# A hybrid decoder step on one core: the last down projection in two passes over token halves

## What is computed

```python
def conv_ffn(h, conv_hist, w_gate, w_up, conv_w, conv_b, w_down):
    gt = h @ w_gate
    ext = jnp.concatenate([conv_hist.astype(gt.dtype), gt], axis=1)
    c = conv_b
    for j in range(CONV_W):
        c = c + ext[:, j:j + L] * conv_w[j]
    f = jax.nn.gelu(c, approximate=True) * (h @ w_up)
    return f @ w_down, ext[:, L:]
...
    f, new_conv = conv_ffn(rmsnorm(x, lp['g_ffn_pre']), ...)
    x = x + rmsnorm(f, lp['g_ffn_post'])
```

## Time and profile before

| | us |
|---|---|
| runs: median of 3 (lowest to highest) | 2643.88 (2643.35 to 2646.94) |
| the profiled execution | 2648.2 |
| its span, first to last instruction | 2646.5 |
| last down projection on PE | 2557.3 to 2605.4 |
| last residual add of DVE ends | 2643.4 |

### The profile page before, as it was taken

How to read it: one execution, slowest core, us unless ns; L and a number is a source line. 1 busy time by engine, 2 the same in 40 slices (tenths; PEclk the granted TensorE clock), 3 DMA queues, 4 the chain that set the end, 5 groups by cost and what they waited for, 6 DMA issues and landing times.

```text
span 2646.5 us, 52869 instructions
## 1 busy us (share of the span) xinstructions
PE 2525.7 (95%) x20496; PEld 2398.3 (91%) x20496; DVE 1127.3 (43%) x1842; ACT 684.2 (26%) x1188; POOL 120.9 (5%) x265
## 2 busy tenths in 40 slices
PE   8999998789899987999999999999999999999994
PEld 8999997555579987999999999999999999999994
DVE  6532313512253339543444344434444444434357
ACT  5211112511022224322222222222222222222231
POOL 3000000000000005000000000000000000000002
PEclk9999998999999998999999999999999999999997
DMA  5478775088864322223323222232323232323231
GB/s 170 133 263 279 274 265 205 1 307 335 320 229 165 87 75 56 85 83 92 88 87 87 87 87 87 87 87 87 87 84 91 87 87 83 91 87 87 83 97 75
DMA packets 146625, 347.36 MB, mean 131 GB/s; under 512 B 16608, under 2 KB 16608, under 8 KB 146048
## 3 DMA queue, kind: packets, MB, share of 16 engines
q1 hardware_dynamic: 144480, 338.35, 39.4%
q0 software_dynamic: 2080, 8.14, 0.8%
HBM read 334.32 MB, written 12.10 MB: 131 GB/s over the span
## 4 chain that ended last, share of the span: by engine, by line
PE 85%; SPq 5%; DVE 4%; DMA 3%; issue 1%; ACT 1%; DVEq 1%; POOL 0%; ACTq 0%
PE ps_acc L719 30%; PE ps_acc L696 15%; PE ps_a L719 15%; PE ps_b L719 15%; PE ps_a L771 4%; SPq L341 3%; SPq L345 1%; DMA region<-vcache 1%; DMA w_raw<-units 1%; PE ps_a L696 1%; PE ps_b L696 1%; PE ps_acc L826 1%; DMA region<-kcache 1%; DVE act_lo L988 1%; PE ps_a L882 1%
## 5 line engine op out<-in xcount | busy, mean ns | idle before, releaser
L270 DVE TENSOR_TENSOR w_lo<-w_raw,w_hi 128x512 fp32r<-128x512 f32 x724 | 500.0, 702 | 1148.6 <-ACT w_hi L264 1144.9
L264 ACT ACTIVATE w_hi<-w_raw 128x512 fp32r<-128x512 f32 x724 | 445.5, 628 | 1432.3 <-PE ps_acc L719 474.6
L719 PE MATMUL ps_acc<-act_hi,w_hi 128*128 128x272 f32 x1472 | 308.9, 292 | 24.7 <-DVE act_lo L988 18.0
L719 PE MATMUL ps_acc<-act_lo,w_hi 128*128 128x272 f32 x1472 | 307.4, 290 | 0.0
L719 PE MATMUL ps_acc<-act_hi,w_lo 128*128 128x272 f32 x1472 | 305.5, 289 | 0.0
L696 PE MATMUL ps_acc<-act_hi,w_hi 128*128 128x272 f32 x1280 | 273.6, 295 | 0.5 <-ACT q_dec L532 0.5
L696 PE MATMUL ps_acc<-act_hi,w_lo 128*128 128x272 f32 x1280 | 264.5, 288 | 0.0
L696 PE MATMUL ps_acc<-act_lo,w_hi 128*128 128x272 f32 x1280 | 264.0, 288 | 0.0
L719 PEld LDWEIGHTS ps_acc<-act_hi,w_hi 128*128 128x128 f32 x1472 | 233.2, 190 | 27.3 <-issue 12.8
L719 PEld LDWEIGHTS ps_acc<-act_hi,w_lo 128*128 128x128 f32 x1472 | 234.1, 190 | 0.0
L719 PEld LDWEIGHTS ps_acc<-act_lo,w_hi 128*128 128x128 f32 x1472 | 233.8, 190 | 0.0
(11 more groups left out here) (217 smaller groups left out, 3725.0 us busy)
## 6 DMA issues: line engine op xcount, KB each, us to landing
w_raw<-units SPq DMA_DIRECT2D x724, 256.0 KB, 2.6
region<-kcache SPq DMA_DIRECT2D x128, 512.0 KB, 4.4
region<-vcache SPq DMA_DIRECT2D x128, 512.0 KB, 7.4
region<-xT SPq DMA_DIRECT2D x8, 544.0 KB, 6.9
region<-xT SPq DMA_DIRECT2D x4, 1088.0 KB, 8.4
yT<-region SPq DMA_DIRECT2D x8, 544.0 KB, 2.7
ext_out<-region POOLq DMA_DIRECT2D x8, 339.5 KB, 3.9
kT_out<-scratch POOLq DMA_DIRECT2D x8, 272.0 KB, 6.4
```

Source lines behind the costliest of these rows:

```text
L264: act.activation(w_hi[:, s], w_raw[:, s], ACT.Copy).then_inc(hi_ready, 1)
L270: dve.tensor_tensor(w_lo[:, s], w_raw[:, s], w_hi[:, s].bitcast(F32), ALU.subtract).then_inc(lo_ready, 1)
L719: mm = pe.matmul(banks(mt, odd)[:, n, 0:HN], w[:, s, i, cols], half(a[:, kt], n), start=kt == 0 and w is w_hi and a is hi, stop=kt == 2 * ...
```

## The change

The last chunk's down projection (16 units) is written out instead of looped, and runs twice, over tokens 0 to 271 and then 272 to 543. In the first pass each unit is split into a place of its own that is kept: the first four in the ring, the other twelve in the space of `act_hi` and `act_lo`, which nobody needs by then. The second pass reads them there. The first pass takes the quarters in pairs (`DOWN`): the four units of `f` tiles 0 and 1 first, then the four of `f` tiles 2 and 3; quarters with even `d` use the first bank of each pair, odd ones the second. The second pass takes them in their old order and uses only the second banks.

All that follows a tile goes by halves too: adds into `acc`, squares (now with four buffers, `sq4`), square sums, root, diagonal, spread and `rstd`. The norm of the first half is placed into the second pass: the sum of squares behind its second unit on PE, the spread behind its fifth; DVE scales and adds the first half's tiles in pairs behind units 6, 8, 10, 12 and 14, and the last three pairs around the second half's norm. POOL's nine adds are gone; DVE makes all of them. SP stores the first half in four transfers of four half tiles and the second in eight of two.

```diff
-Y_POOL = (1, 2, 4, 5, 7, 8, 10, 11, 13)
+DOWN = (0, 1, 4, 5, 2, 3, 6, 7, 8, 9, 12, 13, 10, 11, 14, 15)
...
+        kept_hi, kept_lo = (a[:, :, :].rearrange("p k n -> p (k n)")[:, 0:16 * 512]
+                            .rearrange("p (u i n) -> p u i n", u=16, i=2) for a in (act_hi, act_lo))
...
+        def kept(k):
+            return (w_hi[:, k], w_lo[:, k]) if k < RING else (kept_hi[:, k], kept_lo[:, k])
+        def keep_hi(act, k):
+            act.wait_ge(w_loaded[k % RING], 16 * (Q_LAST + k // RING + 1))
+            act.wait_ge(unit_used, 4 * Q_LAST if k >= RING else 4 * Q_LAST + k - RING + 1)
+            act.activation(kept(k)[0], w_raw[:, k % RING], ACT.Copy).then_inc(hi_ready, 1)
+        def keep_lo(dve, k):
+            dve.wait_ge(hi_ready, 4 * Q_LAST + k + 1)
+            dve.tensor_tensor(kept(k)[1], w_raw[:, k % RING], kept(k)[0].bitcast(F32), ALU.subtract)\
+                .then_inc(lo_ready, 1)
+        def down_at(k, h):
+            d, j = divmod(k if h else DOWN[k], 4)
+            return d, j // 2, j % 2, 0 if h == 0 and d % 2 == 0 else 1
...
-            for k in range(4 * Q_CH - RING):
+            for k in range(4 * Q_CH - 16 - RING):
                 load_unit(sp, (NCH - 1) * Q_CH + Q_FF, k + RING)
+            for k in range(16):
+                load_unit(sp, Q_LAST, k, place=DOWN[k])
+            for i in range(4):
+                sp.wait_ge(y_ready, 4 * i + 4)
+                sp.dma_start(yT[:, 4 * i:4 * i + 4, 0:HN], x2[:, 4 * i:4 * i + 4, 0:HN]).then_inc(y_stored, 16)
             for i in range(KT // 2):
-                sp.dma_start(yT[:, 2 * i:2 * i + 2], x2[:, 2 * i:2 * i + 2]).then_inc(y_stored, 16)
+                sp.wait_ge(y_ready, KT + 2 * i + 2)
+                sp.dma_start(yT[:, 2 * i:2 * i + 2, HN:NT], x2[:, 2 * i:2 * i + 2, HN:NT]).then_inc(y_stored, 16)
...
+            def last_squares(h, m):
+                act.wait_ge(mix_out, (1 + h) * KT + m + 1)
+                if m >= 4 or h:
+                    act.wait_ge(sq_added, (3 + h) * KT + m - 3)
+                act.activation(sq4[:, m % 4], half(acc[:, m], h), ACT.Square).then_inc(sq_done, 1)
+            def last_down(h):
+                for k in range(16):
+                    if h == 0 and k + LEAD < 16:
+                        keep_hi(act, k + LEAD)
+                    d, u, i, n = down_at(k, h)
+                    if u == 1:
+                        for mt in range(2):
+                            last_squares(h, 4 * d + 2 * i + mt)
+                    if h == 1 and k == 2:
+                        root(4)
...
+            def last_down(h):
+                for k in range(16):
+                    d, u, i, n = down_at(k, h)
+                    g = 8 * h + 2 * d + i
+                    hi, lo = kept(k if h == 0 else DOWN.index(k))
+                    if h == 0:
+                        pe.wait_ge(lo_ready, 4 * Q_LAST + k + 1)
+                    for j in range(2):
+                        kt = 2 * u + j
+                        if h == 0:
+                            pe.wait_ge(f_split, (NCH - 1) * CH + kt + 1)
+                        for mt in range(2):
+                            if kt == 0:
+                                pe.wait_ge(acc_free, 2 * (G_LAST + g) + mt + 1 - (8 if 2 <= g < 8 else 4))
+                            for w, a in ((hi, f_hi), (hi, f_lo), (lo, f_hi)):
+                                mm = pe.matmul(banks(mt, i)[:, n, 0:HN], w[:, j, mt * P:(mt + 1) * P], half(a[:, kt], h),
+                                               start=kt == 0 and w is hi and a is f_hi, stop=kt == CH - 1 and w is lo)
+                            if kt == CH - 1 and mt == 0:
+                                mm.then_inc(acc_done, 1)
+                    mm.then_inc(unit_used, 1)
+                    if h == 1 and k == 1:
+                        sum_squares(4, 4 * KT, range(0, 4))
+                    if h == 1 and k == 4:
+                        spread_half(4, 0)
...
+            def half_rstd(n, h):
+                dve.wait_ge(spread_done, n)
+                for i in range(2):
+                    dve.tensor_copy(half(rstd, h)[:, i * HN // 2:(i + 1) * HN // 2], ps[:, i, 0, HN:HN + HN // 2])
+                dve.drain().then_inc(rstd_ready, 1)
...
+            def last_tiles(h, k):
+                d, u, i, n = down_at(k, h)
+                for mt in range(2):
+                    m = 4 * d + 2 * i + mt
+                    tile_done(dve, G_LAST + 8 * h + 2 * d + i, mt, Q_LAST + 4 * h, k)
+                    t = half(acc[:, m], h)
+                    dve.tensor_tensor(t, t, banks(mt, i)[:, n, 0:HN], ALU.add).then_inc(acc_free, 1)
+                    dve.drain().then_inc(mix_out, 1)
+            def add_squares(h, g):
+                for mt in range(2):
+                    m = 2 * g + mt
+                    dve.wait_ge(sq_done, (3 + h) * KT + m + 1)
+                    dve.tensor_tensor(half(sq_sum, h), half(sq_sum, h), sq4[:, m % 4], ALU.add).then_inc(sq_added, 1)
+                    dve.drain()
+            def outputs(h, kts):
+                for kt in kts:
+                    t = half(acc[:, kt], h)
+                    dve.scalar_tensor_tensor(t, t, g_fpost[:, kt:kt + 1], half(rstd, h), ALU.mult, ALU.mult)
+                dve.drain()
+                for kt in kts:
+                    dve.tensor_tensor(half(x2[:, kt], h), half(acc[:, kt], h), half(x2[:, kt], h), ALU.add)\
+                        .then_inc(y_ready, 1)
...
-            for kt in range(KT):
-                dve.scalar_tensor_tensor(acc[:, kt], acc[:, kt], g_fpost[:, kt:kt + 1], rstd[:, :],
-                                         ALU.mult, ALU.mult).then_inc(scaled, 1)
-                if kt not in Y_POOL:
-                    dve.drain()
-                    dve.tensor_tensor(x2[:, kt], acc[:, kt], x2[:, kt], ALU.add).then_inc(y_ready, 1)
+            dve.memset(sq_sum, 0.0)
+            for k in range(16):
+                if k + LEAD < 16:
+                    keep_lo(dve, k + LEAD)
+                d, u, i, n = down_at(k, 0)
+                if u == 1:
+                    last_tiles(0, k)
+                    if 2 * d + i:
+                        add_squares(0, 2 * d + i - 1)
+            add_squares(0, 7)
+            for k in range(16):
+                d, u, i, n = down_at(k, 1)
+                if u == 1:
+                    last_tiles(1, k)
+                    if 2 * d + i:
+                        add_squares(1, 2 * d + i - 1)
+                if k == 2:
+                    mean_square(4, slice(0, 4))
+                if k == 3:
+                    root_mean(4, slice(0, 4))
+                    half_rstd(4, 0)
+                if k >= 6 and k % 2 == 0:
+                    outputs(0, (k - 6, k - 5))
+            add_squares(1, 7)
+            outputs(0, (10, 11))
+            mean_square(5, slice(4, 8))
+            outputs(0, (12, 13))
+            root_mean(5, slice(4, 8))
+            outputs(0, (14, 15))
+            half_rstd(5, 1)
+            for kt in range(0, KT, 2):
+                outputs(1, (kt, kt + 1))
...
-            for kt in Y_POOL:
-                pool.wait_ge(scaled, KT // 2 + kt + 1)
-                pool.tensor_tensor(x2[:, kt], acc[:, kt], x2[:, kt], ALU.add).then_inc(y_pool, 1)
```

More of the change, by code:

```diff
@@ L1273, in _ @@
             root_mean(2)
+            whole_rstd(2)
             def resid(kt):
@@ L1375, in down @@
                                 o.then_inc(acc_free, 1)
-                                if last:
-                                    dve.drain().then_inc(mix_out, 1)
-                    if last:
-                        for i in range(4):
-                            m = 4 * d + i
-                            dve.drain()
-                            dve.wait_ge(sq_done, m + 3 * KT + 1)
-                            dve.tensor_tensor(sq_sum, sq_sum, sq[:, i % 2], ALU.add).then_inc(sq_added, 1)
-                if last:
-                    dve.memset(sq_sum, 0.0)
-                with dve.Fori(0, 3 if last else 4) as d:
-                    down(d, 4)
-                if last:
-                    down(3, 1)
+                if not last:
+                    with dve.Fori(0, 4) as d:
+                        down(d)
+            def last_tiles(h, k):
[20 more added lines that the diff above has]
+                        .then_inc(y_ready, 1)
             chunk(0, first=True)
```

98 lines of the change are left out of this document (51 added, 47 removed).

## The result

| | before | after |
|---|---|---|
| median of 20 runs, us | 2646.57 (2639.1 to 2652.88) | 2651.32 (2643.27 to 2659.14) |
| ratio to before, 95% interval | 1 | 1.0022 [1.0012, 1.0031] |
| profiled execution: time, span, us | 2648.2, 2646.5 | 2648.51, 2646.8 |
| end of f_lo to the end of VectorE's last add, us | 79.5 | 85.8 |
| from there to the end of the span, us | 3.1 | 2.6 |

A forecast was written before the change was run, and what follows sets the result against it. DVE was taken as bound: 74.8 us of work plus 9.3 of waits from 2563.9, 3.1 for the store, 0.5 and 0.7 extra give a span of 2652.3, 5.8 over. On the median 2643.9 that forecasts 2649.7 us, range 2642 to 2658.

The forecast's parts named there:

- The bound: Last down projection and tail: DVE, not PE, sets the end; the question is whether DVE has room.
- The sum of DVE's work: From the last gate tile's low half to DVE's last add: clear, splits, adds, norm chains and outputs, together 74.8 us.
- The first stop of PE: Before the first pass's fourth unit, PE stands 3.3 us for DVE's clear and first split.
- The waits: DVE's waits in both passes, at splits, the second pass's third unit and the first half's spread: together 9.3 us.
- a drop of the clock: Half clock for a while after PE's first gap, beside the first units: 0.7 us on DVE's chain, from 0 to 2.3.
- The unexplained issue gap: In the longer unrolled tail, a gap like the unexplained 0.50 before the square adds: 0.5 us, from 0 to 1.5.
- The store: Behind DVE's last add, the half-size last store (272 KB) still takes 3.1 us, 3.0 at the least.
- the two extras: Costs outside the count of DVE's work and waits: 0.5 us for the unexplained gap and 0.7 for the clock.
- PE as bound: Faster rival: DVE keeps up, PE ends the projection at 2606.4, median 2630.6 us (-0.5%); chance 0.05.
- Cheaper halves: No-change rival: half-width DVE ops within SBUF cost 0.35 us, some 8.5 us go, 2641 us (-0.1%); chance 0.09.
- Half the clock through the second pass: Slower rival: PE's waits in every quarter keep it at the lower clock, 10.9 us a quarter, 2662 us (+0.7%); chance 0.12.
- The signs named ahead: Profile after: DVE nearly unbroken to about 2648, PE idle 3.3 us, ending near 2621, half ops 0.43 to 0.44 us.

The follow-up runs named there:

- e2: Changed kernel without the first half's sixteen gain-and-norm scalings on DVE: 81.1 us from f_lo to DVE's last add, 0.9994 of the time before.
- e1: Changed kernel without the third product (low weights by high activations) in both passes: 85.2 us from f_lo to DVE's last add, 1.0023 of the time before.
- e4: Changed kernel with ten of sixteen weight units split during the last gate tiles and the square-sum clear earlier: 85.1 us from first matmul, 0.9992 of the time before.
- e3: Changed kernel with the first half's norm spread behind the second pass's seventh unit instead of its fifth: 82.6 us from f_lo, 1.0003 of the time before.
- e9: Kernel before, still one pass, with ScalarE multiplying by the gain and DVE's outputs two whole tiles wide: 74.1 us from f_lo, 0.9981 of the time before.
- e8: Changed kernel with early splits, late spread, merged ops, gain multiplied on ScalarE and outputs four half tiles wide: 69.7 us from f_lo, 0.9964 of the time before.
- e6: Changed kernel with square adds, some second-pass tile adds and residual adds joined two tiles at a time: 83.1 us from f_lo, 1.0014 of the time before.

## Why the prediction was right

**The bound.** Right: every wait of PE in the two passes is for DVE, 11.5 us in all, and e2 and, with the reserve on its clock, e1 agree. The question it put, whether DVE has room and not whether PE has, decided the case.

**The sum of DVE's work.** Forecast 74.8 us. The measured stretch less its waits is 85.8 - 10.7 = 75.1. Step by step: half tile adds 0.57 apart (forecast 0.57), square adds 0.55 (0.53), splits 0.63 (0.61), a pair of outputs 1.69 (1.68).

**The first stop of PE.** Forecast 3.3 us, measured 3.1.

**The waits.** Forecast 9.3 us, measured 10.7. For splits 1.41, 1.06 and 1.33 against 1.6, 1.0 and 1.6; at the third unit of the second pass 1.99 against 2.0; at the spread 1.34 and 3.19 against 1.0 and 2.1; two of 0.2 were not forecast.

**The clock, mis-placed.** The prediction put a drop of the clock behind the first stop and gave it 0.7 us. It came at the spread instead. Stretches of the kernel after:

```profile
2558.40:2564.00 5.60, 4.40 (x35) 4.40 (x36) 3.99 (x9) 1.97 (x5) 0.00 (x0) 1.00 0.52 180
...
2594.00:2596.00 2.00, 0.49 (x2) 0.49 (x3) 1.09 (x5) 0.01 (x1) 0.00 (x0) 0.89 0.00 0
2596.00:2598.00 2.00, 2.00 (x11) 2.00 (x10) 0.51 (x2) 0.00 (x0) 0.00 (x0) 0.50 0.04 8
2598.00:2600.00 2.00, 2.00 (x14) 2.00 (x14) 0.00 (x0) 0.00 (x0) 0.00 (x0) 0.76 0.00 0
```

The 3.1 us stop ends in the first of these, at 2559.6, and the clock stays at 1.00 (2.4 GHz); in 2596 to 2598 it is at 0.50 (1.2 GHz). There the spread's four matmuls take 1.25 us, not the 0.6 that the prediction gave them, and DVE's two waits are 1.4 us over the forecast; with the full clock at this place (e2, e4) they are 0.82 and 2.13, near the forecast 1.0 and 2.1. So twice the size allowed for, in another place, within the 0 to 2.3 us kept for it. The place is no property of the code: e2, the same up to there, had half the clock behind the first stop (0.50 in 2566 to 2572), and e3 at neither.

**The unexplained issue gap.** 0.5 us was kept for one. No wait on issue stands among DVE's in the kernel after; the term was 0.

**The store.** The prediction kept 3.1 us behind the last add and 3.0 at the least; it is 2646.8 - 2644.2 = 2.6. The bound was drawn from landing times of 256 and 544 KB, which differ by 0.1 us, but the 256 KB are loads. By the kernel after's trace stores of 272 KB land in 2.2 us, 0.5 less than the 2.7 of the 544 KB stores before, and the end of the kernel came as much sooner.

**What evened out.** The work is 0.3 over the forecast, the waits 1.4, the two extras 1.2 under what was kept for them, the store 0.5 under: 5.8 us in all, as forecast. The mechanism was right; that the total fits to 0.1 us is luck, since the waits came out too long and the two extras and the store too short, by amounts that cancel.

**The rivals.** PE as bound: it would have had PE end the projection 42.5 us behind f_lo (2606.4 less 2563.9); PE ended 59.4 us behind, later even than the 57.7 of the forecast. Cheaper halves: the rows by line and shape of the kernel after say 0.44 us.

```profile
L1490 DVE SCALAR_TENSOR_TENSOR region<-region,gain,rstd 128x272 f32<-128x272 f32 x32 | 14.6, 496 | 0.8
L1484 DVE TENSOR_TENSOR scratch<-scratch 128x272 f32<-128x272 f32 x32 | 14.2, 444 | 3.6
L1493 DVE TENSOR_TENSOR region<-region 128x272 f32<-128x272 f32 x32 | 12.7, 439 | 1.2
```

Half the clock through the second pass: one drop of some 3.4 us instead. The waits for banks that should have fed it were there (2.7 us in three and 0.9 in one, over both passes), and the clock stood at 1.00 from 2600 to the projection's last matmul.

**The signs named ahead.** Ten of the first half's outputs were done before the last tiles and six behind; the first half's last store was issued at 2630.1 and landed 3.1 us later, 11.0 us before the last add; half adds took 0.43 to 0.44 us; PE's first stop was 3.1 us. All as said, but for PE's end, 1.7 us later than its sign.

## What to carry over

Before a tail is moved beside matmuls, count what the engine of the tail already does beside them: here halving the tail's width doubled 64 instructions, each with its fixed cost, and the 26 us that were to be hidden came back as the pace of the passes. Put what can run ahead (the splits) ahead of the point where everyone waits, and the consumer of a small chain (the spread) as late as its reader allows: these two brought 7.3 and 3.2 us, an estimated 1.6 us of each from a fall of the clock that did not come. Before an experiment's gain is put down to its edit, set the granted clock of both executions side by side. And measure a shared job with the helper taken away, since the helper may slow the one it helps.

## What the hardware showed

**GpSimd's adds slowed DVE.** Nine adds of 544 elements on GpSimd, 1802 ns each, made DVE's own adds 1405 instead of 722 ns on average and its scalings 1042 instead of 780. Within the kernel before, the five of DVE's seven adds that ran beside them took 1.67 to 1.68 us, the first and the last 0.73. ScalarE's sixteen multiplications over the same data, in e9, left DVE's instructions at 1.28 to 1.29 us.

**The fixed part of a DVE instruction.** Additions within SBUF took 439 ns at 272 elements, 726 at 544 and 1293 at 1088: 1.05 ns an element and some 154 ns besides. Doubling 64 instructions costs 64 x 0.154 = 9.9 us by that. The Trainium skill, page "VectorE: DVE Perf Modes", section "The TRN2 errata — SBUF-src ops pay a fixed extra latency per instruction", gives a formula for an fp32 add beside its table, (N + 151)/0.96 ns: 441, 724 and 1291 at the three widths. The rows agree with it, not with the table, on which the prediction drew and which has 344 at 272. Its advice of 512 elements or more is in line with e8 and e9, whose wider instructions shortened the stretch; in e6 the wider square adds waited for two squares and brought less.

**The clock.** Stops of 3.1 us passed at 1.00 in the kernel after and in e3, and one as long was followed by half the clock in e2. The stop of 1.8 us at the spread was followed by half the clock in the kernel after and passed at 1.00 in e2 and e4. In e1, whose stops were longer in sum, it fell again and again and stood at 0.68 on average, where the kernel after has 0.86. The Trainium skill, page "TensorE: Matmul & The Clock Gate", section "A second HAM failure mode: psum-queue depth-cycling", tells of such falling and rising between bursts of matmuls; e1 agrees, the kernel after shows one fall only. What chooses the stop stays open.
